# Hybrid attention layer on one core: the attention stage with values as weights, probabilities of four heads as the moving operand, and its query tiles run from the last to the first

## The chip, the cores and the metric

The kernel runs on 1 core of one Trainium2 chip. The metric is the device time of one execution in microseconds (us). Below, PE is TensorE (PEld its weight loads), DVE is VectorE, ACT is ScalarE, POOL is GpSimd, SP is SyncE, which here only issues DMAs.

## The reference, cut to what matters

One layer: a prompt of 1024 tokens and eight sequences that decode one token each. The change is in the attention of the prompt. For each query tile of 128 tokens, each of 8 heads (2 groups of 4 that share keys and values) and three branches, it computes a masked softmax over keys and multiplies by values; the three results are weighted by gates and summed.

```python
s_c = einsum('sghd,ngd->sghn', qg, kcb) * scale         # 63 compressed keys
p_c = masked_softmax(s_c, ...); o_c = einsum('sghn,ngd->sghd', p_c, vcb)
s_s = ... keys 0 .. query (all blocks are chosen at this length)
s_w = ... keys of the last 512 positions
o = g[..., 0:1] * o_c + g[..., 1:2] * o_s + g[..., 2:3] * o_w
mix = concat([o, retention_out], -1) @ w_out            # then the feed-forward part
```

## The kernel before, in words

Five stages follow one another, each a block with a barrier at its end: `stage_project` (twice), `stage_sequences` (the decoding sequences, and the compressed keys and values), `stage_attention` (the prompt's attention, here "the attention stage"), `stage_mix_out`, `stage_feed_forward`. There is no scheduler: each engine has its own list of instructions, written in order, with waits on semaphores.

The attention stage walks over *units*. A unit is one query tile, one head and one branch (compressed: 64 keys wide; selected: tile t has t+1 key tiles of 128; window: up to 5 key tiles). `attention_events` writes one order that all engines follow: S (scores of a unit, PE), T (transposes of up to four key tiles of one unit's probabilities, PE), V (values, PE). Behind S come the row maximum on DVE (`TENSOR_REDUCE`, L1683) and the exponential with its sum on ACT (L1618); behind T a copy of the transposed probabilities to SBUF, in turn on DVE (L1689) and ACT (L1633). In V the transposed probabilities are the weights (128x128, f32) and 64 columns of values move (L1586); f32 makes two PE instructions of each such product. The scores (L1554) are products of fp32r halves: a number is split into `hi` (ACT, L404) and `lo = x - hi` (L408). Each tile's outputs are scaled by gate / sum on POOL (L1661), summed over branches on DVE (L1712), transposed once more on PE (L1568) and kept in `mixT`. Banks: three sets for scores, 5 and 6 for T, 7 for V.

`keep_busy` (L400) issues products whose result nobody reads, at places where PE is about to wait.

## Time and profile before

| | |
|---|---|
| median of 3 runs | 2206.36 us (2204.49 to 2211.82) |
| the profiled execution | 2208.68 us, span of its instructions 2207.0 us |
| busy: PE, DVE, ACT, POOL | 2133.6, 775.0, 610.8, 467.1 us |
| PE instructions | 13245 |
| mean granted TensorE clock | 0.977 of 2.4 GHz |

PE is busy for almost the whole span. Busy time of PE is the union of modelled, overlapping intervals; what one instruction costs is read from the distance between starts.

### The profile page before, as it was taken

The numbers are of one execution on the slowest core, as the hardware profiler recorded it, in microseconds if no ns is written. First come the engines' busy times: TensorE is split into PE (matmuls) and PEld (weight loads), VectorE is DVE, ScalarE is ACT, GpSimd is POOL, SyncE is SP. The second block draws the span as 40 slices with busy tenths as digits, with TensorE's granted clock in tenths as the row PEclk, the third lists the DMA queues.
The fourth block names the chain that finished last, engine by engine and source line by source line (L and its number), as shares of the span: only waits on it lengthen the run. The fifth ranks groups of instructions, "written<-read, shape, count | busy, mean of one in ns | idle before, by whom it ended". The sixth has DMA issues, their size and how long they took to land. (4 is left out here: it accounts for less than half of the span.)

```text
span 2207.0 us, 35846 instructions
## 1 busy us (share of the span) xinstructions
PE 2133.6 (97%) x13245; PEld 1889.4 (86%) x13245; DVE 775.0 (35%) x1460; ACT 610.8 (28%) x1282; POOL 467.1 (21%) x424
## 2 busy tenths in 40 slices
PE   6999999989999999899999999999999999999998
PEld 5777768867777677789999998799999999999987
DVE  5544433554244444453544553301111011111015
ACT  4310111111343333354555552222110111111112
POOL 0111111212222331210100002133321333223330
PEclk9999989999999999986999999999999999999999
DMA  6211102247796774340000003221111111111123
GB/s 176 67 59 39 39 11 98 68 105 128 111 122 90 102 101 59 70 106 11 14 18 1 1 18 117 68 73 42 47 48 48 48 48 43 43 48 48 45 69 116
DMA packets 173859, 141.54 MB, mean 64 GB/s; under 512 B 16601, under 2 KB 160682, under 8 KB 173410
## 3 DMA queue, kind: packets, MB, share of 16 engines
q1 hardware_dynamic: 169634, 131.43, 26.0%
q0 software_dynamic: 4096, 8.40, 2.5%
q8 instruction: 80, 1.31, 0.3%
q14 instruction: 49, 0.40, 0.1%
HBM read 124.27 MB, written 19.69 MB: 65 GB/s over the span
## 5 line engine op out<-in xcount | busy, mean ns | idle before, releaser
L393 PE MATMUL banks<-halves 128*128 128x344 f32 (+4 forms) x5184 | 849.8, 326 | 2.5 <-POOL halves L408 2.5
L393 PEld LDWEIGHTS banks<-halves 128*128 128x128 f32 (+1 forms) x5184 | 816.4, 187 | 31.3 <-issue 2.8
L408 POOL TENSOR_TENSOR halves<-core,halves 128x1024 fp32r<-128x1024 f32 (+1 forms) x143 | 243.7, 1712 | 632.9 <-ACT halves L404 482.9
L393 PE MATMUL banks<-hidden 128*128 128x512 f32 (+3 forms) x1512 | 347.3, 385 | 4.3 <-DVE hidden L408 4.3
L393 PEld LDWEIGHTS banks<-hidden 128*128 128x128 f32 (+1 forms) x1512 | 252.8, 178 | 72.0 <-issue 4.6
L1065 PE MATMUL banks<-arena 128*128 128x254 f32 (+1 forms) x1152 | 245.3, 368 | 7.8 <-ACT arena L1201 7.8
L1065 PEld LDWEIGHTS banks<-arena 128*128 128x128 f32 x1152 | 206.4, 191 | 32.8 <-issue 6.1
L404 ACT ACTIVATE halves<-core 128x1024 fp32r<-128x1024 f32 (+1 forms) x85 | 88.0, 1047 | 389.5 <-PE banks L393 369.6
L1586 PE MATMUL banks<-kept,softmax 128*128 128x64 f32 (+1 forms) x1184 | 183.5, 289 | 7.8 <-ACT softmax L1633 4.9
L2046 DVE TENSOR_TENSOR core<-banks,core 128x344 f32<-128x344 f32 x66 | 34.1, 517 | 440.6 <-PE banks L393 440.6
L1586 PEld LDWEIGHTS banks<-kept,softmax 128*128 128x128 f32 (+1 forms) x1184 | 162.1, 203 | 17.6 <-issue 10.5
L1618 ACT ACTIVATE softmax<-banks,softmax 128x64 f32<-128x64 f32 (+8 forms) x192 | 109.4, 571 | 135.0 <-DVE softmax L1683 127.3
L1683 DVE TENSOR_REDUCE softmax<-banks 128x1 f32<-128x640 f32 (+4 forms) x184 | 102.4, 558 | 105.7 <-PE banks L1558 105.0
L1554 PE MATMUL banks<-pairs 128*128 128x128 f32 (+3 forms) x592 | 116.3, 325 | 1.3 <-DVE pairs L408 1.3
L966 POOL DMA_DIRECT2D arena<-in_cache_kv x128 | 67.8, 530 | 231.3 <-PE banks L1111 203.3
L1574 PE MATMUL banks<-core,softmax 128*128 128x128 f32 (+1 forms) x592 | 115.7, 292 | 0.0
L1554 PEld LDWEIGHTS banks<-pairs 128*128 128x128 f32 x592 | 99.3, 209 | 4.1 <-issue 1.5
L603 POOL TENSOR_TENSOR retention<-core,retention 128x256 f32<-128x256 f32 (+1 forms) x36 | 30.3, 842 | 260.9 <-ACT core L586 260.9
L400 PE MATMUL banks<-core 128*128 128x128 f32 x576 | 75.4, 297 | 9.9 <-PEq L132 3.8
L1689 DVE COPY softmax<-banks 64x128 f32<-64x128 f32 (+4 forms) x129 | 59.4, 460 | 72.5 <-PE banks L1574 71.8
L400 PEld LDWEIGHTS banks<-core 128*128 128x128 f32 x576 | 73.6, 212 | 10.7 <-issue 9.9
L1574 PEld LDWEIGHTS banks<-core,softmax 128*128 128x128 f32 (+1 forms) x592 | 77.3, 161 | 4.2
(213 smaller groups left out, 1887.3 us busy)
## 6 DMA issues: line engine op xcount, KB each, us to landing
core<-in_cache_kv SPq DMA_DIRECT2D x128, 128.0 KB, 5.5
core<-in_w_gate SPq DMA_DIRECT2D x22, 512.0 KB, 3.8
core<-in_w_up SPq DMA_DIRECT2D x22, 512.0 KB, 3.8
core<-in_x_prompt SPq DMA_DIRECT2D x16, 512.0 KB, 3.6
arena<-in_cache_kv SPq DMA_DIRECT2D x128, 64.0 KB, 5.5
arena<-in_cache_kv POOLq DMA_DIRECT2D x128, 64.0 KB, 5.3
retention<-in_w_in SPq DMA_DIRECT2D x16, 448.0 KB, 6.4
core<-in_w_down SPq DMA_DIRECT2D x16, 448.0 KB, 3.7
```

What stands on the lines that cost most here:

```text
L393: done = pe.matmul(out, left[a], right[b], start=(first and i == 0), stop=(last and i == 2))
L400: pe.matmul(m.banks[:, bank, 0:P], m.ident, m.ident, start=True, stop=True)
L404: return act.activation(hi, x, ACT.Copy)
L408: return engine.tensor_tensor(lo, x, hi.bitcast(F32), ALU.subtract)
L966: pool.dma_start(m.selv[16 * at:16 * at + 16, half, :, :], io.pool[bass.ds(page[pg], 1), :, :, 384:512].rearrange("a c t n -> (a c) t n")) ...
L1065: last = pe.matmul(m.banks[:, 2 + mt, 0:2 * nb], m.w1[kv][:, k, P * mt:P * mt + P], m.XT[:, k % 8, :, k // 8:k // 8 + nb], start=(k == 0), ...
L1554: last = pe.matmul(out[:, lo:hi], m.qs[t % 2][:, g, hh, :], pair[v][:, first + lo:first + hi], start=(v == 0), stop=(v == 1 and not mask))
L1574: last = pe.transpose(m.banks[0:w, 5 + i % 2, P * x:P * x + P], m.prob[u % 4][:, P * (first + x):P * (first + x) + w], m.ident)
L1586: last = pe.matmul(m.banks[:, 7, HD * (u % 8):HD * (u % 8) + HD], m.pts[i % 3][0:w, P * x:P * x + P], v[0:w, 64 * g:64 * g + 64], start=(f ...
L1618: act.activation(m.prob[i % 4][:, 0:width(i)], scores_of(i, width(i)), ACT.Exp, bias=m.nmax[:, i % 8:i % 8 + 1], accum_out=m.sums[UNITS[i] ...
L1683: dve.tensor_reduce(peak, out, AX.X, ALU.max, negate=True).then_inc(s["c_max"], 1)
L1689: dve.tensor_copy(m.pts[i % 3][0:w, 0:P * n], m.banks[0:w, 5 + i % 2, 0:P * n]).then_inc(s["c_kept_dve"], 1)
```

## The change

1. **Values as weights.** A turn (T) now takes one key tile of the four heads of a group: four transposes fill one bank with 512 columns. ACT rounds it to `hi`, DVE takes `lo`. V then has the weights `[value_hi | value_lo]` (128x128) and moves 512 columns twice (`hi`, `lo`). Bank 7 adds up all three branches of a group.
2. **Weights on the probabilities.** 1/sum and gate are multiplied into the probabilities before they are transposed, on POOL (`weigh`), per quad (four heads of one group and branch). The scaling of outputs, the sum over branches and the last transpose go; instead one half of bank 7 is copied by ACT, one by DVE, and POOL adds them.
3. **Order.** Units go (tile, group, branch, head), tiles from 7 to 0. Scores run 8 units ahead instead of 3, in two bank pairs (0-1, 2-3) instead of three; T uses banks 4 to 6, V runs two turns behind T.
4. **Preparation moved.** Splitting keys, the first two query tiles and the values, and the query loads, go from the start of the attention stage to the end of `stage_sequences`.
5. **All `keep_busy` calls are removed**, 288 products in 13 places of the run.

```diff
+VALUES = 2 * TP * 256 + 256
+PAIRS_C = 8 * SEQ + 2 * SEQ + 3 * 2 * 512 + VALUES
-UNITS = [(t, hh, g, br) for t in range(TP) for hh in range(4) for g in range(2) for br in range(3)]
-AHEAD = 3
-BANK_C = [4, 0, 2]
+UNITS = [(t, g, br, hh) for t in range(TP) for g in range(2) for br in range(3) for hh in range(4)]
+AHEAD = 8
+QUADS = len(UNITS) // 4
+def tile_at(x):
+    return TP - 1 - x
...
+    for k in range(QUADS):
+        n = key_tiles(4 * k)
+        for x in range(n):
+            turns.append((k, x, n))
+            events.append(("T", len(turns) - 1))
+            if len(turns) > 2:
+                values(len(turns) - 3)
+            while ahead < min(len(UNITS), AHEAD + 4 * k + -(-4 * (x + 1) // n)):
+                events.append(("S", ahead))
+                ahead += 1
...
     PE
-                    wait(pe, "c_exp", i - 2)
+                    wait(pe, "c_exp", i - 1)
...
+                    wait(pe, "c_lo", i - 2)
+                    pe.wait_ge(s["c_shared"], 4 * k + 4)
+                    for hh in range(4):
+                        last = pe.transpose(m.banks[0:w, 4 + i % 3, P * hh:P * hh + P],
+                                            m.prob[(4 * k + hh) % 12][:, P * x:P * x + w], m.ident)
...
-                        last = pe.matmul(m.banks[:, 7, HD * (u % 8):HD * (u % 8) + HD],
-                                         m.pts[i % 3][0:w, P * x:P * x + P], v[0:w, 64 * g:64 * g + 64],
+                    pe.wait_ge(s["c_lo"], i + 1)
+                    if br == 0:
+                        wait(pe, "c_out_act", k // 3)
+                        wait(pe, "c_out_dve", k // 3)
+                    for half in range(2):
+                        last = pe.matmul(m.banks[:, 7, :], v.rearrange("p v d -> p (v d)"), m.pts[i % 3][half][0:w, :],
...
     ACT: at S(i) exponent(i - 1); at T(i)
+                    act.wait_ge(s["c_turned"], i + 1)
+                    wait(act, "c_pv", i - 2)
+                    round_to_hi(act, m.pts[i % 3][0][0:w, :], m.banks[0:w, 4 + i % 3, :]).then_inc(s["c_hi"], 1)
...
     POOL
+                for hh in range(4):
+                    u, gate = 4 * k + hh, 12 * g + 3 * hh + br
+                    p = m.prob[u % 12][:, 0:width(u)]
+                    pool.tensor_scalar(p, p, m.share[t % 2][:, u % PER_TILE:u % PER_TILE + 1],
+                                       m.gates[:, tile_at(t), gate:gate + 1], ALU.mult, ALU.mult).then_inc(s["c_shared"], 1)
...
+                    if i % 4 == 1 and i >= 5:
+                        weigh((i - 5) // 4)
...
     DVE
+                    if i % 4 == 1 and i >= 5:
+                        inverse((i - 5) // 4)
+                    peak(i)
+                    low_halves()
...
     end of stage_sequences, on DVE (the three others stand before the copy to osm)
+                        dve.wait_ge(s["c_keys_hi"], 4)
+                        rest_to_lo(dve, m.keys[1][1][1], m.kstage[1][1], m.keys[1][1][0]).then_inc(s["c_keys_lo"], 1)
...
-                if q + 2 not in SEQS_B:
-                    keep_busy(pe, m, 2, 26 if q < NB_SEQ else 38)
...
-            keep_busy(pe, m, 7, 22)
```

On PE, in the attention stage before, for the last group of heads but one of tile 7 (L1574 is T, L1586 is V, L1554 and L1558 are S):

```order
1622 L1586 MATMUL banks<-kept,softmax 128x64
1623 L1574 MATMUL banks<-core,softmax 128x128 x4
1624 L1554 MATMUL banks<-pairs 128x512 x2
1625 L1554 MATMUL banks<-pairs 128x384 x2
1626 L1554 MATMUL banks<-pairs 128x128 x2
1627 L1558 MATMUL banks<-kept 128x128
1628 L1586 MATMUL banks<-kept,softmax 128x64
1629 L1574 MATMUL banks<-core,softmax 128x128 x4
1630 L1586 MATMUL banks<-kept,softmax 128x64 x4
```

After the change, on PE, in the first selected quad of tile 7 (L1561 is T, L1575 is V, L1549 and L1553 are S):

```order
638 L1561 MATMUL banks<-core,arena 128x128 x4
639 L1575 MATMUL banks<-pairs 128x512 x2
640 L1561 MATMUL banks<-core,arena 128x128 x4
641 L1575 MATMUL banks<-pairs 128x512 x2
642 L1549 MATMUL banks<-kept_pairs,pairs 128x64 x2
643 L1553 MATMUL banks<-kept 128x64
644 L1561 MATMUL banks<-core,arena 128x128 x4
645 L1575 MATMUL banks<-pairs 128x512 x2
646 L1561 MATMUL banks<-core,arena 128x128 x4
647 L1575 MATMUL banks<-pairs 128x512 x2
```

Four products of 64 moving columns have become two of 512 for four heads, and scores of the next compressed quad stand between every second pair of turns.

On POOL after the change, from the end of `stage_sequences` into tile 7 (L401 is the split to `lo`, L1627 `weigh`, L1649 the sum of a group's halves):

```order
634 L1009 CAST kept<-arena 128x128 x2
635 L401 TENSOR_TENSOR pairs<-arena,pairs 64x1024
636 L401 TENSOR_TENSOR pairs<-kept,pairs 128x16x64 x2
637 L401 TENSOR_TENSOR pairs<-kept,pairs 64x2x64
638 L401 TENSOR_TENSOR pairs<-arena,pairs 64x1024
...
642 L1627 TENSOR_SCALAR arena<-arena,kept 128x64 x4
643 L1627 TENSOR_SCALAR arena<-arena,kept 128x1024 x4
644 L1627 TENSOR_SCALAR arena<-arena,kept 128x640 x4
645 L1627 TENSOR_SCALAR arena<-arena,kept 128x64 x4
646 L1627 TENSOR_SCALAR arena<-arena,kept 128x1024 x4
647 L1649 TENSOR_TENSOR core<-core,arena 64x4x128
```

The splits of queries and values now stand ahead of the barrier, and each quad's probabilities pass through POOL.

## Rows read from the trace of the kernel before

**Rows 1.** The page: span, and granted clock in 40 slices of 55 us.
```profile
span 2207.0 us, 35846 instructions
...
PEclk9999989999999999986999999999999999999999
```

**Rows 2.** Busy time in the attention stage with its two ends (columns as named).
```profile
core 0: us, PE busy (x) PEld busy (x) DVE busy (x) ACT busy (x) POOL busy (x), PEclk, DMA share, GB/s
938.00:1316.00 378.00, 367.02 (x2901) 349.62 (x2902) 187.15 (x366) 194.95 (x556) 38.97 (x15) 0.92 0.09 22
```

**Rows 3.** The same inside the attention stage.
```profile
955.00:982.00 27.00, 25.28 (x216) 23.42 (x215) 15.81 (x58) 18.20 (x83) 5.11 (x2) 0.98 0.68 163
982.00:1036.00 54.00, 54.00 (x267) 51.46 (x266) 18.07 (x43) 21.25 (x69) 5.11 (x2) 0.51 0.06 17
1036.00:1310.00 274.00, 267.90 (x2269) 255.64 (x2269) 140.72 (x256) 147.63 (x392) 23.25 (x9) 1.00 0.02 7
```

**Rows 4.** Timeline of DVE: the instruction that closes a query tile, here tiles 0, 6, 7.
```profile
973.24 0.16 DVE L1695 TENSOR_SCALAR softmax<-softmax 128x24 f32<-128x24 f32 x1
...
1252.46 0.16 DVE L1695 TENSOR_SCALAR softmax<-softmax 128x24 f32<-128x24 f32 x1
...
1309.17 0.18 DVE L1695 TENSOR_SCALAR softmax<-softmax 128x24 f32<-128x24 f32 x1
```

**Rows 5.** Timeline of PE in tile 7: start, duration, line, count.
```profile
1291.00 1.23 PE L1554 MATMUL banks<-pairs 128*128 128x512 f32 x6
...
1292.23 0.43 PE L1586 MATMUL banks<-kept,softmax 64*128 64x64 f32 x2
1292.60 1.09 PE L1574 MATMUL banks<-core,softmax 128*128 128x128 f32 x8
1293.45 0.42 PE L1554 MATMUL banks<-pairs 128*128 128x128 f32 x2
...
1294.42 1.95 PE L1586 MATMUL banks<-kept,softmax 128*128 128x64 f32 x16
1296.21 0.28 PE L1574 MATMUL banks<-core,softmax 128*128 128x128 f32 x1
```

**Rows 6.** Busy time in 4 us of dense fp32r products of 512 columns (projection).
```profile
328.00:332.00 4.00, 4.00 (x19) 3.20 (x19) 1.47 (x3) 0.60 (x1) 1.14 (x2) 1.00 0.03 13
```

**Rows 7.** Groups by line and shape, DVE and ACT: count, busy us, mean ns.
```profile
L1683 DVE TENSOR_REDUCE softmax<-banks 128x1 f32<-128x640 f32 x40 | 33.0, 825 | 31.4 <-PE banks L1558 31.3
L1683 DVE TENSOR_REDUCE softmax<-banks 128x1 f32<-128x1024 f32 x8 | 9.8, 1223 | 7.0 <-PE banks L1558 7.0
L1618 ACT ACTIVATE softmax<-banks,softmax 128x640 f32<-128x640 f32 x40 | 31.7, 793 | 38.0 <-DVE softmax L1683 38.0
L408 DVE TENSOR_TENSOR halves<-banks,halves 128x512 fp32r<-128x512 f32 x16 | 10.2, 680 | 0.0
L404 ACT ACTIVATE halves<-banks 128x512 fp32r<-128x512 f32 x16 | 8.5, 582 | 0.0
```

**Rows 8.** The same for POOL: copies, and a subtraction of two tensors.
```profile
L986 POOL COPY arena<-core 128x2048 f32<-128x2048 f32 x16 | 32.0, 2010 | 98.7 <-DMA core<-in_cache_kv 70.3 <-PE banks L1044 28.4
L606 POOL COPY kept<-core 128x128 f32<-128x128 f32 x16 | 5.1, 318 | 0.0
L408 POOL TENSOR_TENSOR halves<-core,halves 128x1024 fp32r<-128x1024 f32 x76 | 182.9, 2408 | 474.4 <-ACT halves L404 474.4
```

**Rows 9.** Timeline where `stage_sequences` ends and the attention stage begins.
```profile
921.24 8.75 PE L400 MATMUL banks<-core 128*128 128x128 f32 x76 [0.36 <-ACT core L1192]
...
926.67 1.28 DVE L1355 TENSOR_SCALAR arena<-arena,core 8x2049 f32<-8x2049 f32 x1
...
936.97 0.22 PE L1117 MATMUL banks<-core,arena 8*128 8x8 f32 x1 [0.37 <-DVE arena L1362]
...
945.49 8.12 DVE L408 TENSOR_TENSOR pairs<-core,pairs 128x1024 fp32r<-128x1024 f32 x4 [7.92 <-ACT pairs L404]
...
955.34 0.27 PE L1574 MATMUL banks<-core,softmax 128*64 128x128 f32 x1
```

**Rows 10.** Timeline from the last V to the first product of `stage_mix_out`.
```profile
1308.54 1.28 PE L1586 MATMUL banks<-kept,softmax 128*128 128x64 f32 x10
...
1320.82 22.04 PE L393 MATMUL banks<-halves 128*128 128x512 f32 x96
```

More of the change, by code:

```diff
@@ L394, in split_products @@
     return done
-def keep_busy(pe, m, bank, n):
-    for _ in range(n):
-        pe.matmul(m.banks[:, bank, 0:P], m.ident, m.ident, start=True, stop=True)
 def round_to_hi(act, hi, x):
@@ L1453, in attention_events @@
[L1453 to L1474 removed]
+    turns, events, ahead = [], [("S", u) for u in range(AHEAD)], AHEAD
@@ L1477, in load_w_out, with turned_by @@
+    values(len(turns) - 2)
+    values(len(turns) - 1)
+    return turns, events
+TURNS_C, EVENTS_C = attention_events()
+def turned_by(k):
+    return sum(quad < k for quad, _, _ in TURNS_C)
 def load_w_out(sp, s, m, io, k):
```

395 lines of the change are left out of this document (170 added, 225 removed).

## The prediction, made before the changed kernel ran

> **What bounds the kernel now.** I read the page first: a span of 2207.0 us with a granted clock that is full nearly everywhere, but falls in two slices of the attention stage [rows 1]. Busy shares say little here, so the second view is busy time by stretch: in the attention stage PE is busy for 367 of 378 us, DVE and ACT for about half of it, POOL for a tenth [rows 2]. The mean clock there is 0.92, and the stretches inside show why: 54 us at 0.51 of 2.4 GHz, that is at the 1.2 GHz level, the rest at 2.4 GHz [rows 3]. So PE sets the pace, and the timeline gives its prices as distances between starts. In tile 7, eight transposes take 1293.45 - 1292.60 = 0.85 us, 0.106 each; sixteen V instructions 1296.21 - 1294.42 = 1.79 us, 0.112 each, and a key tile of a head needs two, 0.224; scores of 1024 keys take 1.23 us, window scores 0.97 us, compressed ones about 0.27 us (my estimate from the two) [rows 5]. Check: tile 7 has 8 x 14 key tiles, 112 x 0.330 = 37.0, plus 8 x 2.47 = 19.8, is 56.8 us; its closing instructions lie 1309.17 - 1252.46 = 56.7 us apart [rows 4]. A pure sum of PE work explains the tile.
>
> From the first T to the last V the stage takes 1309.3 - 955.3 = 354 us [rows 9, 10]. The 54 us at 1.2 GHz do the work of 27, so at full clock it would be 327. The PE sum over all eight tiles is 592 x 0.330 = 195, scores about 115 (from the prices above, falling with width to 0.3 for one key tile), last transposes 4: 314. The stage runs 4% above its sum.
>
> **V.** Removed are 592 x 0.224 = 132.6 us. Added are 148 turns x 2 products of 512 fp32r columns. The projection shows 19 such in 4.00 us, 0.21 each [rows 6]: 62.2 us. Transposes stay 592, scores stay. The last transposes and their wait go, -4. PE's own work at full clock falls from 327 to 327 - 70 - 4 = 253 us. On path, since PE was the bound.
>
> **The other engines get close.** A turn costs ACT a split of 512 columns (0.58) and DVE a subtraction (0.68); before, half the turns fell on each [rows 7]. For tile 7, DVE has 28 x 0.68 = 19, maxima 8 x (1.22 + 0.83 + 0.22) = 18, reciprocals and output copies 3: 40 us. ACT has 28 x 0.58 = 16, exponentials 8 x (1.12 + 0.79 + 0.31) = 18, others 2: 36. PE has 11.9 + 11.8 + 19.8 = 43.5. None exceeds PE, yet three engines at 80 to 100% that wait for one another in a fixed order don't overlap fully. Where I see waits:
> - Window scores now come four in a row behind the compressed turn, in two bank pairs, and S(i) waits for the exponential of i-2. One loop is 0.97 + 0.83 + 0.79 and some 0.2 of signals, 2.8 us for two, 1.4 each against 0.97: 1.7 us per group of heads, less for narrow tiles, 1.5 x 16 = 24 us. Queued behind the waiting S are the first transposes of the selected quad, and behind them ACT and DVE.
> - In the selected quad DVE takes a turn's low half behind the maximum of the next score, and T(i+2) waits for that half. Per two turns: max 0.22, low 0.68, T 0.44, V 0.42, S 0.27, signals 0.3, is 2.3 against 2.0 of PE work: 0.15 x 72 turns = 11 us.
> - The first V of a group waits until both halves of bank 7 are copied (about 0.6 us) with only one T ahead of it: 0.5 x 16 = 8 us.
> - `weigh` on POOL is an operation no row shows: one tensor and two per-partition factors. Nearest is POOL's copy, also of one tensor: 2.01 us for 2048, 0.32 for 128 columns, so 1.1 for 1024; the far bound is the subtraction of two tensors, 2.41 [rows 8]. Nothing lets it cost less than a copy. It lies on the path once a group: for the selected quad it starts some 2.65 us after that quad's last scores (max 1.22, exponential 1.12, signals and reciprocal), and PE has 7.3 us of other work until it needs the result (two turns 1.7, four window scores 5.6). At the copy's price 2.65 + 4 x 1.1 = 7.1: hidden, barely. At the subtraction's, 12.3: 5 us per group in tile 7. I take the copy's, since the engine reads one tensor, and 5 us in all for what doesn't fit.
>
> The Trainium skill (GPSIMD Engine Reference, 3.1) gives about 2.6 cycles per element with two inputs and 1.8 at 1.2 GHz as best for a tight loop; by the latter, an estimate from that page, 1024 columns would take some 1.7 us and the total would be about 11 us higher. The copy in this trace is faster than that page's 1.8, and the subtraction's 2.4 us agree with its 2.6.
>
> Stage: 253 + 24 + 11 + 8 + 5 = 301 against 354, -53 us. This includes that the long 1.2 GHz stretch isn't repeated (27 us of it): it began on narrow tile 1 and ended as the tiles grew wider, and the new order begins with wide ones. That part is the least certain.
>
> **Preparation moved.** Before, T begins at 955.34, 18.4 us after PE's last work of the stage ahead, most of it behind DVE's four splits of keys (8.12 us) [rows 9]. After, those run in the tail of `stage_sequences`. They aren't free: the last selected exponential stands behind four splits on ACT (+1.2), DVE does a split ahead of the last output copy (+1.4 to 2.1), POOL subtracts two query and two value tiles, 2.4 each, starting about 928 when ACT gives the first: its end is near 942 instead of 937. On the other side the transposes that waited for `keep_busy` until 929.99 could start at 927.95 (-2.0). First S at about 942.7. Eight scores before the first T cost some 4 us more than their PE work, a cold start 3, the first `weigh` 1: -5 us net. The drain of the last quads adds 4.
>
> **The idle-time products.** 288 x 0.23 = 66 us of PE time go, but nearly all lay in waits, so I count none as gain but the 2.0 above. The one ahead of that, 26 products, hid nothing and kept the clock: without it PE idles 6 us and the following 7 us of work may run at 1.2 GHz, +3. At the start of `stage_mix_out` PE waits for POOL's first low half as before: 11.0 us from last V to first product [rows 10] become 2.7 (copy, sum, barrier) + 4.9 + 3 cold = 10.6: 0. The other places: cold start against an earlier start, 0; if that cover is missing, 1 to 3 us each for six places.
>
> **Sum.** -53 - 5 + 4 + 3 + 0 = -51. The profiled execution took 2208.7; 2157.7. The runs' median lies 2.3 below it: 2156 us.
>
> **The rivals.**
> - *Clock, slower than before.* PE stops several times per group now. At 1.2 GHz tile 7's PE work is 87 us against 51 forecast, so each us spent there loses about 0.4. The forecast gain is used up by some 120 us more at 1.2 GHz than I assume. For it: before, the clock fell within tile 1 and stayed low for 54 us though PE was 100% busy there [rows 3], and nothing fills the waits now. Against: wide tiles ran at 2.4 GHz for 274 us, the work was narrow where it fell, and V now moves 512 columns for each load. If it decides: 2215 to 2260. 12%. The Trainium skill (TensorE: Matmul & The Clock Gate, 1) says idle gaps cool the engine; that the clock fell behind waits here agrees.
> - *POOL at the two-tensor price.* 5 us per group in tile 7 falling to nothing in tile 0 is 40 us, and the window quad adds 2 for eight groups: about +50, 2205 us, no change. 8%.
> - *Waits hidden.* If running 8 ahead hides nearly all waits, the stage takes its PE sum, 255 to 265: 2115 us. 10%.
> - *The forecast*, 2120 to 2190: 67%. The rest (3%) is spread.
>
> **How the numbers follow.** A difference of 0.3%, about 7 us, is what the measurement can tell. Faster: 67 + 10 and half of what ends between 2190 and 2205, 5, is 82%; same 5%; slower 13%. The range 2110 to 2210 takes in the two-tensor bound and the hidden case and leaves out the clock rival and a little below.
>
> **What would show it.** V: 296 instructions at distances of 0.21 us, tile 7 in about 51 us. Scores: starts of consecutive window scores 1.4 us apart, PE released by ACT. `weigh`: 1.1 us for 1024 columns; a PE wait on POOL ahead of the first selected transposes would prove it longer. Clock: a row of 0.5 inside tiles 7 to 3 would prove me wrong. The boundary: first S near 943, last V near 1256. The forecast fails most likely if PE's waits are longer than these loops, or if the clock follows them.

## The result, and the profile after

The changed kernel takes 2200.02 us (median of 11 runs, 2198.84 to 2206.69), the kernel before 2207.79 us in the same rounds (11 runs, 2204.09 to 2213.43). The ratio is 0.9966 with a 95% interval of 0.9954 to 0.9979: faster by 0.34%, some 7.5 us, where the forecast was 51. The time lies in the range, but the likeliest case was wrong by 44 us. Its profiled execution took 2200.3 us. In the rounds of some later experiments five executions of the kernel before took only 2179 to 2185 us, at a mean granted clock of 0.990 to 0.993 where the others have 0.975 to 0.983; that is some 27 us less, about what its low stretch costs (none of the five has a trace), and it widens several of the intervals below.

On the page of the changed kernel, TensorE's busy time and the granted clock in 40 slices (before: [rows 1]):

```profile
PE 2037.4 (93%) x11749; PEld 1762.2 (80%) x11749; DVE 810.0 (37%) x1526; ACT 642.4 (29%) x1290; POOL 597.8 (27%) x628
...
PEclk9999989988999999789889769999999999999999
```

The attention stage begins in the 18th slice and ends in the 24th. The kernel before showed two slices below 9 there, now there are five, and a sixth just ahead of the stage. Busy time by stretch, with the sum of PE's instructions in parentheses behind it and the granted clock third from the end, here from the first T to the last V:

```profile
core 0: us, PE busy (x) PEld busy (x) DVE busy (x) ACT busy (x) POOL busy (x), PEclk, DMA share, GB/s
955.10:1300.70 345.60, 297.00 (x1794) 252.94 (x1793) 205.71 (x418) 213.29 (x541) 153.96 (x209) 0.85 0.05 14
```

The same tile by tile, 7 to 0 (each stretch ends where GpSimd adds the last group of the tile, L1649):

```profile
955.00:1022.70 67.70, 57.09 (x363) 49.55 (x361) 42.21 (x70) 42.77 (x92) 27.29 (x31) 0.90 0.14 37
1022.70:1076.20 53.50, 47.87 (x302) 41.22 (x300) 34.66 (x62) 34.89 (x78) 22.99 (x28) 0.88 0.04 11
1076.20:1127.80 51.60, 46.77 (x283) 39.83 (x281) 32.16 (x59) 32.19 (x76) 22.09 (x28) 0.85 0.04 11
1127.80:1171.20 43.40, 37.80 (x249) 32.22 (x249) 29.16 (x58) 29.82 (x74) 21.28 (x28) 0.96 0.08 25
1171.20:1207.90 36.70, 29.27 (x208) 25.59 (x208) 24.47 (x53) 25.60 (x70) 19.56 (x28) 1.00 0.01 2
1207.90:1245.70 37.80, 32.15 (x188) 27.80 (x188) 19.75 (x50) 22.44 (x66) 17.84 (x28) 0.77 0.00 1
1245.70:1279.30 33.60, 28.44 (x148) 24.09 (x148) 15.43 (x49) 17.33 (x61) 13.70 (x27) 0.70 0.00 1
1279.30:1301.00 21.70, 17.72 (x61) 12.73 (x61) 8.16 (x28) 8.65 (x32) 9.20 (x18) 0.50 0.00 1
```

From these rows the whole miss can be worked out. The length of a stretch is PE's busy time and its idle time. The busy time multiplied by the granted clock is what the same work takes at 2.4 GHz, the rest of it is what the low clock costs. Summed over the eight tiles, this is 252.4 us of work at 2.4 GHz, 44.8 us for the clock and 48.9 us of idle time; by the one row ahead of them it is 252.5, 44.6 and 48.6, the numbers used below. The forecast had 253 of work, 48 of waits and nothing for the clock. (The clock has two decimals, so each such product is good to 1 or 2 us.) The kernel before, by the row from its first T to its last V (354.50 us, PE busy for 346.68, clock 0.92), spends 318.9, 27.7 and 7.8 us. So V's cheaper form returns 66 us, the waits take 41 back and the clock 17 more.

How a fall of the clock looks from close by: TensorE in stretches of 2 us in tile 6, where a group of heads changes.

```profile
1038.00:1040.00 2.00, 1.60 (x12) 1.52 (x12) 0.94 (x2) 1.58 (x3) 0.00 (x0) 1.00 0.00 0
1040.00:1042.00 2.00, 1.02 (x10) 0.91 (x8) 1.95 (x4) 0.89 (x2) 0.35 (x1) 1.00 0.00 0
1042.00:1044.00 2.00, 1.74 (x13) 1.64 (x14) 1.08 (x2) 0.92 (x3) 2.00 (x3) 0.94 0.00 0
1044.00:1046.00 2.00, 0.94 (x5) 0.75 (x3) 0.82 (x1) 0.84 (x2) 1.94 (x2) 0.50 0.00 0
1046.00:1048.00 2.00, 1.91 (x8) 1.75 (x8) 0.00 (x0) 0.60 (x1) 0.00 (x0) 0.50 0.03 8
1048.00:1050.00 2.00, 2.00 (x10) 1.38 (x8) 1.59 (x4) 1.91 (x5) 1.11 (x1) 0.50 0.00 0
```

PE is busy for 1.60, 1.02 and 1.74 of 2 us, and at 1043.8 us the level falls to 1.2 GHz. It holds to 1054.0: through one more wait of 1.15 us, for GpSimd, and 8 us in which PE is fully busy. Such waits are paid twice: once as idle time, once as slow work behind them. In steps of 0.25 us the level falls seven times in tiles 7 to 4. Four times (965.3, 992.5, 1019.8 and 1074.5 us) this comes at the end of a wait of 1.3 to 2.1 us for GpSimd or within 2 us behind it; three times (here, at 1098.3 and at 1146.3) it comes ahead of that wait, behind waits of scores for ScalarE. Not every wait is paid twice: tile 3 has the largest share of idle time of all eight, 7.4 of 36.7 us, in waits of 1.0 us at most, and its clock is 1.00. Who ends these waits, from the waits of PE between 940 and 1310 us (in total, times, longest):

```profile
PE banks L1549 <- ACT arena L1593: 27.9, 51, 1.4
PE banks L1561 <- POOL arena L1627: 16.9, 21, 2.1
PE banks L392 <- POOL halves L401: 7.3, 1, 7.3
PE banks L1549 <- PEq L890: 3.5, 1, 3.5
PE banks L1575 <- DVE pairs L401: 2.4, 7, 0.6
PE banks L1561 <- DVE pairs L401: 2.0, 2, 1.0
```

Scores (L1549) wait for the exponential (L1593), the first selected turn (L1561) for `weigh` (L1627). The price of `weigh`, the operation that no row of before showed, from the groups by shape (count, then busy us and mean ns):

```profile
L1627 POOL TENSOR_SCALAR arena<-arena,kept 128x640 f32<-128x640 f32 x40 | 34.4, 874 | 15.3 <-DVE arena L1679 14.7
L1627 POOL TENSOR_SCALAR arena<-arena,kept 128x64 f32<-128x64 f32 x64 | 24.0, 393 | 87.9 <-DVE arena L1679 87.9
...
L1627 POOL TENSOR_SCALAR arena<-arena,kept 128x1024 f32<-128x1024 f32 x8 | 9.4, 1195 | 13.6 <-DVE arena L1679 13.6
```

1.195 us for 1024 columns: near the copy's price (1.1 taken), far from the subtraction's 2.41. The Trainium skill (GPSIMD Engine Reference, 3.1) has 1.8 cycles per element as the best case of a tight loop, from which I had estimated 1.7 us. From 64 to 1024 columns the rows give 0.84 ns a column, 1.0 cycle at that section's 1.2 GHz; that disagrees with the 1.8 and is near the 1.03 that the same section has for bodies bound by the read and write ports. The measurement decides.

### The profile page after: what moved, and what is told of

The parts are those of the page before. It is cut to its first block and busy times, and to the rows that moved or that the text cites. A ratio compares the mean times of both kernels' runs of the same rounds, so it can differ in the third digit from the quotient of the medians.

```text
span 2198.6 us, 32717 instructions
## 1 busy us (share of the span) xinstructions
PE 2037.4 (93%) x11749; PEld 1762.2 (80%) x11749; DVE 810.0 (37%) x1526; ACT 642.4 (29%) x1290; POOL 597.8 (27%) x628
## 5 line engine op out<-in xcount | busy, mean ns | idle before, releaser
L401 POOL TENSOR_TENSOR halves<-core,halves 128x1024 fp32r<-128x1024 f32 (+1 forms) x143 | 243.8, 1713 | 575.5 <-ACT halves L397 425.6
L1085 PE MATMUL banks<-arena,blocks 128*128 128x254 f32 (+1 forms) x1152 | 248.1, 372 | 9.7 <-ACT arena L1219 5.7
L1085 PEld LDWEIGHTS banks<-arena,blocks 128*128 128x128 f32 x1152 | 209.2, 194 | 35.1 <-issue 6.1
L2037 DVE TENSOR_TENSOR core<-banks,core 128x344 f32<-128x344 f32 x66 | 34.1, 517 | 439.8 <-PE banks L392 439.8
L1627 POOL TENSOR_SCALAR arena<-arena,kept 128x64 f32<-128x64 f32 (+8 forms) x192 | 122.2, 652 | 164.2 <-DVE arena L1679 162.9
L1668 DVE TENSOR_REDUCE arena<-banks 128x1 f32<-128x64 f32 (+8 forms) x184 | 102.3, 556 | 103.1 <-PE banks L1553 102.5
L1549 PEld LDWEIGHTS banks<-pairs 128*128 128x128 f32 x592 | 103.0, 204 | 36.7 <-issue 27.1
L1549 PE MATMUL banks<-pairs 128*128 128x128 f32 (+3 forms) x592 | 109.2, 315 | 20.8 <-ACT arena L1593 20.5
L1593 ACT ACTIVATE arena<-banks,arena 128x64 f32<-128x64 f32 (+8 forms) x192 | 109.1, 568 | 60.1 <-DVE arena L1668 56.2
L1575 PE MATMUL banks<-pairs 128*128 128x512 f32 (+1 forms) x296 | 122.5, 500 | 3.4 <-DVE pairs L401 2.4
L1561 PE MATMUL banks<-core,arena 128*128 128x128 f32 (+1 forms) x592 | 107.2, 311 | 19.0 <-POOL arena L1627 16.9
L397 ACT ACTIVATE pairs<-banks 128x512 fp32r<-128x512 f32 (+1 forms) x148 | 88.3, 596 | 85.3 <-PE banks L1561 84.6
L401 DVE TENSOR_TENSOR pairs<-banks,pairs 128x512 fp32r<-128x512 f32 (+1 forms) x148 | 100.0, 680 | 9.9 <-ACT pairs L397 9.9
L1561 PEld LDWEIGHTS banks<-core,arena 128*128 128x128 f32 (+1 forms) x592 | 74.5, 157 | 28.3 <-issue 18.9
```

The source lines that it names most:

```text
L397: return act.activation(hi, x, ACT.Copy)
L401: return engine.tensor_tensor(lo, x, hi.bitcast(F32), ALU.subtract)
L1085: last = pe.matmul(m.banks[:, 2 + mt, 0:2 * nb], m.w1[kv][:, k, P * mt:P * mt + P], m.XT[:, k % 8, :, k // 8:k // 8 + nb], start=(k == 0), ...
L1549: last = pe.matmul(out[:, lo:hi], m.qs[t % 2][:, g, hh, :], pair[v][:, first + lo:first + hi], start=(v == 0), stop=(v == 1 and not mask))
L1561: last = pe.transpose(m.banks[0:w, 4 + i % 3, P * hh:P * hh + P], m.prob[(4 * k + hh) % 12][:, P * x:P * x + w], m.ident)
L1575: last = pe.matmul(m.banks[:, 7, :], v.rearrange("p v d -> p (v d)"), m.pts[i % 3][half][0:w, :], start=(br == 0 and half == 0), stop=(br ...
```

## The experiments

All ratios are to the kernel before, run on the same chip in the same rounds; its medians there lie between 2207.4 and 2210.4 us. The experiments are compared with one another and with the changed kernel (2200.02 us) by their medians, across rounds. For each kernel the stretch from the first T to the last V is split as above, in its one profiled execution. Where idle-time products stand inside the loop, they are part of the work. The profiled execution of `earlier` is the shortest of ten (2200.0 us), that of earlier_fill the longest of four (2187.9 us), so their splits look better and worse than their medians.

| kernel | us, median | ratio, 95% interval | first T to last V | work at 2.4 GHz | clock | idle |
|---|---|---|---|---|---|---|
| before | 2207.79 | 1 | 354.5 | 318.9 | 27.7 | 7.8 |
| changed | 2200.02 | 0.9966, 0.9954 to 0.9979 | 345.6 | 252.5 | 44.6 | 48.6 |
| bare_before | 2228.49 | 1.0092, 1.0063 to 1.012 | 370.3 | 316.8 | 47.3 | 6.1 |
| old_fill | 2215.25 | 1.0028, 1.0012 to 1.0043 | 345.2 | 253.3 | 41.2 | 50.7 |
| first_to_last | 2208.15 | 1.0, 0.9983 to 1.0017 | 355.3 | 254.9 | 48.5 | 51.9 |
| fill_inside | 2182.86 | 0.9897, 0.9862 to 0.9932 | 328.8 | 293.9 | 9.1 | 25.8 |
| fill_half | 2181.82 | 0.9911, 0.987 to 0.9952 | 330.0 | 281.2 | 18.0 | 30.8 |
| fill_both | 2174.59 | 0.9874, 0.9833 to 0.9914 | 328.0 | 283.4 | 11.8 | 32.8 |
| weigh_short | 2163.65 | 0.9858, 0.9751 to 0.9965 | 308.2 | 252.2 | 21.9 | 34.1 |
| spread | 2261.72 | 1.0312, 1.0199 to 1.0425 | 403.7 | 248.9 | 66.2 | 88.7 |
| earlier | 2210.56 | 1.0019, 0.999 to 1.0047 | 344.7 | 253.6 | 37.9 | 53.2 |
| dve_one | 2207.75 | 1.0003, 0.9977 to 1.0029 | 349.6 | 252.5 | 44.6 | 52.5 |
| earlier_fill | 2182.31 | 0.9896, 0.9831 to 0.9962 | 338.1 | 282.7 | 21.3 | 34.1 |
| earlier_dve_fill | 2186.85 | 0.9907, 0.9877 to 0.9936 | 337.2 | 284.5 | 15.0 | 37.7 |
| prompt | 2167.75 | 0.985, 0.9798 to 0.9902 | 313.6 | 251.0 | 21.8 | 40.7 |
| prompt_fill | 2164.56 | 0.9828, 0.9759 to 0.9897 | 316.4 | 278.0 | 11.6 | 26.8 |
| prompt_fill_win | 2159.02 | 0.9804, 0.9735 to 0.9873 | 308.2 | 269.5 | 8.3 | 30.4 |
| banks4 | 2199.55 | 0.9948, 0.9924 to 0.9972 | 345.6 | 248.3 | 47.3 | 50.0 |
| prompt_banks4 | 2162.21 | 0.978, 0.9758 to 0.9802 | 307.1 | 247.6 | 15.8 | 43.7 |
| best | 2155.62 | 0.9763, 0.9743 to 0.9783 | 307.4 | 262.4 | 13.8 | 31.2 |

The work column is the check on the method: in the ten kernels that have the changed loop and no products in it, it is 248 to 255 us, while the stretch itself takes 307 to 404 us. What differs is the clock and the waits.

The expectations speak of "low-clock time": the time at the 1.2 GHz level, which is 2 x (1 - clock) x length. For the changed kernel it is 2 x 0.15 x 345.6, about 104 us (the expectations say 103).

**bare_before: the kernel before without its idle-time products.**

```
 def keep_busy(pe, m, bank, n):
-    for _ in range(n):
-        pe.matmul(m.banks[:, bank, 0:P], m.ident, m.ident, start=True, stop=True)
+    return
```

> The kernel before with all of its idle-time products (288 of them) left out and nothing else changed. Theory A (the chip lowers TensorE's clock where TensorE waits often or long, and these products kept it up at the stage boundaries): low-clock rows appear behind the boundaries and in stage_mix_out, and the time rises by 6 to 20 us to 2214 to 2228. Rival N (my forecast: the products were worth nothing): within 3 us of before, 2205 to 2211. The attention stage itself has no such products between its first and last turn, so by both it stays near 354 us from first T to last V.

Slower by 0.92%, some 20 us: my zero for these products was wrong. Most of the loss is where I did not look. First T to last V takes 370.3 us instead of 354.5, although none of the products taken out stood in that stretch; both readings had it unchanged. By stretch:

```profile
942.00:1051.00 109.00, 97.62 (x476) 92.33 (x477) 43.12 (x108) 47.40 (x161) 15.68 (x6) 0.50 0.23 57
1051.00:1326.00 275.00, 268.87 (x2274) 256.49 (x2273) 141.56 (x257) 148.30 (x393) 23.25 (x9) 1.00 0.03 7
...
955.70:1051.00 95.30, 95.30 (x467) 90.42 (x468) 34.26 (x100) 41.11 (x153) 10.22 (x4) 0.50 0.23 56
```

Without the products at the entry of the stage the clock is at the 1.2 GHz level for 109 us from the first score on, with PE busy for 97.6 of them, and from the first T on (the last row) for all 95.3; in [rows 3] it was 54. So a low clock is not only a matter of the gap just ahead: once low, it stayed low through the narrow tiles 0 and 1 and into tile 2 although PE was never idle, and rose as the tiles grew wide.

**old_fill: the changed kernel with the products at their old places.**

```
+            keep_busy(pe, m, 7, 38)
             for what, i in EVENTS_C:
+                if (what, i) == ("T", 0):
+                    keep_busy(pe, m, 7, 18)
...
+            keep_busy(pe, m, 7, 22)
             for i in range(NT + 1):
```

> The changed kernel with the idle-time products put back at all places where the kernel before had them, none inside the attention loop. Theory A: the granted clock inside the attention stage stays near 0.85, since its waits are not filled; the stretch 1300 to 1431 goes from 0.91 back to 1.00 and stage_sequences from 0.95 to 0.98; the time falls by 8 to 16 us, to 2184 to 2192. Rival N: 2197 to 2203. Rival O (the low clock inside the attention stage is a consequence of how it is entered): the stage's clock rises to 0.92 or more and the time falls by over 20 us, to below 2180.

It is slower than without them, against all three readings, and the timeline of PE at the entry of the stage says why:

```profile
942.65 0.22 PE L1151 MATMUL banks<-core,arena 8*128 8x8 f32 x1 [3.40 <-DVE arena L1411]
947.80 11.41 PE L399 MATMUL banks<-core 128*128 128x128 f32 x76 [4.93 <-PEq L900]
...
968.75 5.07 PE L399 MATMUL banks<-core 128*128 128x128 f32 x36
```

The 38 products (76 records, two to a product) take 11.4 us, the 18 ahead of the first T 5.1 us. The wait of 18 us that they filled in the kernel before is gone, since the preparation was moved, so 16 us of them lie on the path. Inside the loop nothing changed (clock 0.86). A product that fills a wait has to go when the wait goes; but from where the first product of `stage_mix_out` runs to the end, this kernel needs 885.9 us instead of the changed kernel's 890.6, so the late ones are worth some 5 us, less 2 by which that first product is itself delayed.

**first_to_last: the order of the tiles alone.**

```
 def tile_at(x):
-    return TP - 1 - x
+    return x
```

> The changed kernel with the query tiles taken from the first to the last again (one line). Theory A: the waits are in every tile, so low-clock stretches appear in the wide tiles again, now late in the stage; order alone is worth less than 8 us: 2192 to 2208. Rival T (it is the order that lowers the clock: narrow tiles in the last 80 us, and a cold start on wide ones): the clock of the stage moves by 0.04 or more and the time by over 15 us, in either direction.

8 us slower than the changed kernel, with nearly the same clock (0.84 against 0.85) and idle time within 4 us.

```profile
954.90:1060.00 105.10, 86.75 (x428) 72.94 (x428) 44.84 (x125) 53.06 (x172) 44.68 (x75) 0.65 0.16 40
1060.00:1310.20 250.20, 216.66 (x1384) 185.83 (x1382) 163.53 (x289) 163.15 (x369) 109.98 (x134) 0.93 0.02 7
```

The order moves the low stretch of the narrow tiles from the end to the start and does not make it. The order is not the cause, and my hope that "the new order begins with wide ones" would save the 27 us was without ground.

**fill_inside and fill_half: products in the loop's waits.**

```
                 if what == "S":
...
+                    keep_busy(pe, m, 4 + turned % 3, {0: 0, 1: 0, 2: 2}[br])
                     wait(pe, "c_exp", i - 1)
...
                 elif what == "T":
...
                     wait(pe, "c_lo", i - 2)
+                    turned = i + 1
+                    if x == 0:
+                        keep_busy(pe, m, 4 + i % 3, (0, 4, 0)[k % 3])
                     pe.wait_ge(s["c_shared"], 4 * k + 4)
```

They write the bank that the next turn will overwrite. fill_half has 1 and 3 in place of 2 and 4.

> The changed kernel with idle-time products inside the attention loop only: 2 ahead of each window score and 4 ahead of the first selected turn of a group, 192 products of 128 columns, 44 us at 2.4 GHz, placed where the trace shows TensorE waiting for ACT and for POOL. Theory A (TensorE's many short waits lower its clock): granted clock of the stage 0.97 or more, the 45 us that the low clock costs come back less some 10 to 20 us of products that do not fit into the waits: 2165 to 2175. Rival W (the clock falls for another cause, such as narrow tiles or load): clock stays near 0.85 and the products cost 10 to 25 us: 2210 to 2225.

> Idle-time products inside the attention loop as in the run with 192 of them, but 1 ahead of each window score and 3 ahead of the first selected turn: 112 products, 26 us at 2.4 GHz. With 192, the low-clock time from first T to last V fell from 103 to 18 us, and 19 of their 44 us lay on TensorE's path. Theory A (short waits lower the clock, and fillers that just fit restore it): low-clock time stays under 30 us, under 8 us of products on the path, time 2168 to 2178. Rival D (the clock needs the whole filling): low-clock time above 60 us, time 2185 to 2198.

This is the direct test of the clock. With 192 products more work and nothing else changed, the kernel is faster by 17 us, and the clock inside the stage shows one low stretch, in the narrow tiles:

```profile
953.40:1247.00 293.60, 272.95 (x2013) 242.03 (x2011) 191.67 (x371) 198.03 (x485) 140.73 (x181) 1.00 0.06 17
1247.00:1282.20 35.20, 30.09 (x167) 25.18 (x166) 14.14 (x47) 15.47 (x57) 14.03 (x29) 0.74 0.00 1
```

The clock's part falls from 44.6 to 9.1 us. The work grows by 41 us (192 products at 0.23 us would be 44); 23 of them went into waits (idle 48.6 to 25.8) and 18 or 19 onto the path. That is within the 10 to 20 expected, but the clock gave back 35.5 us and not all 45, and the time lies 8 us above the range. With 112 products the clock holds less well (18.0) and less lies on the path (28.7 us more work, 17.8 less idle time): the same time, between the two readings. So idleness was the cause of the falls in the wide tiles, and filling is a dear cure.

**fill_both: with products at the ends of the neighbouring stages.** fill_half, and `keep_busy` as before in `values` (26 and 38), 14 in place of 22 at the start of `stage_mix_out`, 14 at its end, 18 at the start of the feed-forward stage.

> The 112 products inside the attention loop as in the run with half the filling, and products where the kernel before had them around the last two values of stage_sequences (26 and 38), at the start (14 instead of 22) and the end (14) of stage_mix_out and at the start of the feed-forward stage (18), none at the start of attention and none in the projections. Theory A: 3 us less up to the first score, 3 us less in stage_mix_out and behind it than the run with the 112 alone. Rival N (these outer products are worth nothing by themselves, as between the kernel before with and without them up to 895 us): the same time as that run within 2 us.

7 us below fill_half by the medians. The two profiled executions differ by 5.0 us: 3.0 from the first product of `stage_mix_out` to the end, 2.0 from the first T to the last V, nothing elsewhere. The products at the end of `stage_sequences` gave nothing by the first T.

**weigh_short: GpSimd's work cut.** Only 64 columns of each row are weighed, the rest is left out.

```
-                    p = m.prob[u % 12][:, 0:width(u)]
+                    p = m.prob[u % 12][:, 0:64]
```

> The changed kernel with GpSimd's weighing of the probabilities cut to the first 64 columns of each score row (the rest stays unweighed, so part of the computation is left out). Theory P (the wait of the first selected turns for GpSimd, 16.9 us in 21 places, is a cause of its own and also starts the clock's falls in the wide tiles): these waits go, low-clock time falls by 20 us or more, time 2165 to 2182. Rival L (another wait of the loop takes their place, the scores' wait for the exponentials above all): 2188 to 2200, with the clock of the stage near 0.85.

```profile
PE banks L1549 <- ACT arena L1593: 28.4, 54, 1.4
...
PE banks L1561 <- POOL arena L1627: 1.9, 4, 0.7
```

The wait for GpSimd falls from 16.9 to 1.9 us, the scores' wait stays. The stage gets 37 us shorter: 15 of idle time and 23 of clock. The time, 2163.65 us, is 1 us below theory P's range. GpSimd's lateness, which I had at 5 us, costs 37. From the first T up to 1150 us the level still falls four times, behind waits of scores, and stays low for 3.3 to 3.5 us each time; in the changed kernel it falls seven times up to there, for 3.3 to 10.3 us.

**spread: the window scores spread over the selected turns.**

```
-            while ahead < min(len(UNITS), AHEAD + 4 * k + -(-4 * (x + 1) // n)):
+            upto = 4 * k + (2 if k % 3 == 0 else -2 + -(-6 * (x + 1) // n) if k % 3 == 1 else -(-4 * (x + 1) // n))
+            while ahead < min(len(UNITS), AHEAD + upto):
```

> The changed kernel with the window scores spread: two of the four behind the compressed turn, the other two and the next compressed scores over the selected turns, instead of four in a row. Theory S (my term of 24 us: four window scores in a row wait for maximum and exponential through two bank pairs, 27.9 us of waits in 51 places): these waits fall to under 12 us, and the time by 8 to 20 us, to 2180 to 2192. Rival P (the first selected turn then comes earlier and waits that much longer for GpSimd's weights): TensorE's wait for GpSimd grows from 17 to 30 us or more, and the time stays within 6 us of 2200.

```profile
PE banks L1562 <- POOL arena L1628: 73.9, 28, 5.6
PE banks L1550 <- ACT arena L1594: 12.7, 26, 1.2
```

The scores' waits fell to 12.7 us, nearly what theory S had, and the time rose by 61 us. The wait for GpSimd grew as in rival P, but to 73.9 us, and the time left P's range as well, which was 2200 within 6 us. The four window scores in a row are the cover under which GpSimd weighs. In the sum, 57 us more waiting for GpSimd and 15 less for ScalarE made 40 us more idle time and 22 more of clock loss.

**earlier and dve_one: two ways to help GpSimd.** `earlier` makes the four selected scores one window turn sooner; `dve_one` gives the fourth selected head to VectorE, behind the maximum of the fourth window score.

```
+            steps = max(1, n - 1) if k % 3 == 2 else n
-            while ahead < min(len(UNITS), AHEAD + 4 * k + -(-4 * (x + 1) // n)):
+            while ahead < min(len(UNITS), AHEAD + 4 * k + min(4, -(-4 * (x + 1) // steps))):
```

```
-                for hh in range(4):
+                for hh in range(3 if br == 1 else 4):
...
                     peak(i)
+                    if i % 4 == 3 and i >= 7 and UNITS[i - 7][2] == 1:
+                        weigh_last((i - 7) // 4)
```

> The changed kernel with the four selected scores of the next group placed one window turn earlier (behind the first turns of the window quad but its last), so that GpSimd starts to weigh them earlier; nothing else. Cutting GpSimd's weighing to 64 columns took 15 us of waits and 54 us of low clock from the stage, 37 us in all; spreading the scores the other way cost 58. Theory P (GpSimd misses its due time by about 1 us a group, and each miss also lowers the clock in the wide tiles): TensorE's wait for GpSimd falls from 17 to under 8 us, low-clock time from 103 to under 75, time 2172 to 2188. Rival R (the earlier scores wait for the exponentials of their own predecessors instead, so the chain starts no earlier): 2196 to 2204.

> The changed kernel with one of the four selected heads weighed by VectorE (behind the maximum of the fourth window score) instead of GpSimd. Theory P: GpSimd's chain is 1.2 us shorter in the widest tile, the wait of the first selected turn for it nearly goes (under 6 us in all) if VectorE is in time, low clock under 75 us, time 2172 to 2190. Rival V (VectorE is the next late one: its 1.1 us ahead of a low half delays turns and the wait moves there): within 6 us of 2200, with the first selected turn waiting for VectorE.

> The earlier selected scores together with the 112 products inside the loop and those at the ends of the neighbouring stages (2174.6 us without the earlier scores). Theory P: once the wait for GpSimd is short, the products ahead of the selected turns do not fit into it any more (48 of them, 11 us), so the two edits do not add up: 2164 to 2174. Rival: they add, the wait gains 10 us or more again: below 2162.

> Earlier selected scores, one selected head weighed by VectorE, and the same products. Theory P: no wait for GpSimd left, and the time of the run without VectorE's share within 5 us, since what it could still remove is under 5 us: 2160 to 2172. Rival V (VectorE's extra 1.1 us a group delays low halves): 5 us or more above the run without it.

None helped: `earlier` and `dve_one` can't be told from the kernel before, their medians are 11 and 8 us above the changed kernel's and outside every range that was put down for them, and with the products they are 8 and 12 us above fill_both. In dve_one the first selected turn waits for VectorE's weighing instead (21.3 us in 16 places), which is the mechanism of rival V. In `earlier` the wait for GpSimd stays at 19.3 us, so how early the scores are made does not set its start. In the changed kernel, the last selected score of the group of the 2 us stretches above, on PE:

```profile
1035.52 1.03 PE L1549 MATMUL banks<-pairs 128*128 128x512 f32 x6
1036.39 0.23 PE L1553 MATMUL banks<-kept 128*128 128x128 bf16 x1
...
1046.09 1.09 PE L1561 MATMUL banks<-core,arena 128*128 128x128 f32 x4 [1.15 <-POOL arena L1627]
```

its exponential on ACT:

```profile
1038.00 0.59 ACT L397 ACTIVATE pairs<-banks 64x512 fp32r<-64x512 f32 x1 [0.31 <-PE banks L1561]
1038.50 0.99 ACT L1593 ACTIVATE arena<-banks,arena 128x896 f32<-128x896 f32 x1
```

the maximum of the first window score, a low half, and only then the reciprocal on DVE:

```profile
1040.05 0.82 DVE L1668 TENSOR_REDUCE arena<-banks 128x1 f32<-128x640 f32 x1 [1.11 <-PE banks L1553]
1040.79 0.67 DVE L401 TENSOR_TENSOR pairs<-banks,pairs 64x512 fp32r<-64x512 f32 x1
1041.39 0.16 DVE L1679 RECIPROCAL arena<-arena 128x4 f32<-128x4 f32 x1
```

and GpSimd:

```profile
1041.65 4.29 POOL L1627 TENSOR_SCALAR arena<-arena,kept 128x896 f32<-128x896 f32 x4 [6.97 <-DVE arena L1679]
```

`weigh` starts 5.2 us after the last instruction of the last selected score (1036.4 to 1041.65). The exponential ends at 1039.5, but its sum is inverted behind a maximum whose score PE has not yet made. The program writes exponential i at event S(i+1) and the reciprocal at the second event S behind the quad, so both hang on the next scores.

**prompt: two places in the queues.** The last selected exponential goes right behind its own score on ScalarE, the reciprocal ahead of the first window score's maximum on VectorE. No work is added or taken away.

```
+def last_selected(u):
+    return UNITS[u][2] == 1 and u % 4 == 3
+def sums_ready(i):
+    if i % 4 == 0 and i and last_selected(i - 1):
+        return i // 4 - 1
+    if i % 4 == 1 and i >= 5 and not last_selected(i - 2):
+        return i // 4 - 1
...
-                    if i:
+                    if i and not last_selected(i - 1):
                         exponent(i - 1)
+                    if last_selected(i):
+                        exponent(i)
...
-                    if i % 4 == 1 and i >= 5:
-                        inverse((i - 5) // 4)
+                    if sums_ready(i) is not None:
+                        inverse(sums_ready(i))
```

> The changed kernel with its scores where they are, but the exponential of the last selected head queued on ScalarE right behind its own score instead of one score later, and the reciprocal (and so GpSimd's weighing) of the selected quad ahead of the first window score's maximum and low half instead of behind them. In the trace the weighing starts 5.2 us after the last selected score, of which 1.7 us is the reciprocal queued behind that maximum and low half. Theory Q (GpSimd is late because its start hangs on a place in the queues, not on when the scores are made, which is why making them earlier changed nothing): it starts 1.3 to 1.8 us earlier, TensorE's wait for GpSimd falls from 17 to under 6 us, low-clock time in the stage from 103 to under 80, time 2170 to 2188. Rival R (ScalarE now stands in that exponential while a turn's high half waits, and the wait moves to the turns): 2195 to 2208.

```profile
PE banks L1563 <- ACT arena L1607: 28.2, 49, 1.4
...
PE banks L1575 <- POOL arena L1643: 6.4, 12, 1.0
```

2167.75 us is 32 us below the changed kernel and 2 us below the range of theory Q. The wait for GpSimd falls from 16.9 to 6.4 us, idle time by 8, and the clock's part from 44.6 to 21.8. Theory Q had the wait under 6 us and the low-clock time under 80 (it is 50). On DVE the reciprocal now stands ahead of the window's maximum, and GpSimd starts behind it, 3.9 us after the last selected score (1032.4 to 1036.3):

```profile
1036.07 0.17 DVE L1695 RECIPROCAL arena<-arena 128x4 f32<-128x4 f32 x1
1036.15 0.80 DVE L1684 TENSOR_REDUCE arena<-banks 128x1 f32<-128x640 f32 x1
```

```profile
1036.34 4.31 POOL L1643 TENSOR_SCALAR arena<-arena,kept 128x896 f32<-128x896 f32 x4 [5.61 <-DVE arena L1695]
```

The two moves were only run together, so what each gives is not known.

**prompt_fill and prompt_fill_win: products on top of it.** The first has all of fill_both, the second the same without the 3 ahead of each first selected turn.

> The same, with the 112 products inside the loop and those at the ends of the neighbouring stages (2174.6 us without the prompt start). Theory Q: what the prompt start takes away was partly filled already, so 2160 to 2170. Rival R: 2174 to 2184.

> The same without the 3 products ahead of each first selected turn (64 products inside the loop). Theory Q: those 48 products (11 us) stood in a wait that is gone, so leaving them out saves 4 to 9 us against the run with them, if the clock holds: 2154 to 2164. Rival (the clock falls without them): equal or above the run with them.

Both in the ranges of theory Q: with GpSimd prompt, the 48 products cost 5.5 us and the clock holds without them.

**banks4, prompt_banks4, best: the score banks.** A score row of up to 512 columns takes one of the four banks, a wider one a pair.

```
-        b = 2 * (u % 2)
-        return m.banks[:, b:b + 2, :].rearrange("p a n -> p (a n)")[:, 0:width(u)]
+        b = BANKS_OF[u]
+        return m.banks[:, b[0]:b[-1] + 1, :].rearrange("p a n -> p (a n)")[:, 0:width(u)]
...
-                    wait(pe, "c_exp", i - 1)
+                    wait(pe, "c_exp", FREE_AT[i])
```

> The changed kernel with score banks given out by width: a score row of up to 512 columns takes one of the four banks instead of a pair, so that up to four such scores are in flight; rows over 512 columns take a pair as before. Theory S (my term of 24 us: scores wait for the exponential two back because there are two pairs): the waits of scores for ScalarE, 28 us, fall to under 15 us, mostly in tiles 3 to 0, whose low clock shortens too: 2182 to 2194. Rival L (another engine's pace sets these tiles, so the wait only moves): 2197 to 2203.

> Banks by width together with the prompt start of GpSimd (2167.8 us without the banks). Theory S: 6 to 16 us less, 2152 to 2162. Rival L: 2165 to 2170.

> Banks by width, the prompt start, the 64 products ahead of window scores and those at the ends of the neighbouring stages (2159.0 us without the banks). Theory S: the products ahead of the window scores no longer stand in waits in the narrow tiles, so less is left to gain: 2150 to 2157. Rival L: 2157 to 2161.

```profile
PE banks L1579 <- POOL arena L1645: 36.0, 23, 2.8
PE banks L1567 <- ACT arena L1611: 12.4, 20, 1.0
```

In banks4 the scores' wait falls from 27.9 to 12.4 us, and the wait for GpSimd rises from 16.9 to 36.0: the time does not move. My term of 24 us was a real wait, but behind it stood another that took it over. With the prompt start the banks give 5.5 us, between the two readings. `best` (banks by width, prompt start, 64 products in the loop, those at the neighbouring stages' ends) takes 2155.62 us, 0.9763 of the kernel before: 2.4% faster and in theory S's range, where the change alone gave 0.34%. That this is the time I forecast for the change is chance.

## Why the prediction was wrong, point by point

**V: right in sum.** The forecast had 253 us of PE work at full clock, the row gives 252.5. V has 296 instructions. But a turn with its two V products takes 0.90 to 0.95 us against my 0.86: its four transposes 0.35 to 0.39 us instead of 0.44, its two products 0.55 instead of 0.42. Over 148 turns that is 6 to 13 us more than forecast, so that the whole fits to 1 us is in part luck; which of the other terms was too high by as much is open.

**The waits: right in sum, wrong in their parts.** 48 us forecast, 48.6 measured, which is luck, since three of the four terms were far off. The scores' wait for ScalarE was 24 and is 27.9. The low halves were 11 and are 4.4 (2.4 and 2.0), the first V of a group 8 and is under 1. GpSimd was 5 and is 16.9. There the step that failed is that "for the selected quad it starts some 2.65 us after that quad's last scores". I added up the durations of its chain and left out what the program's order puts ahead of the exponential and the reciprocal on their engines; it starts 5.2 us after them. The price per row, over which I drew the rival of 8%, was right (1.195 us for 1024 columns), so POOL's late start did what its price did not.

**The clock: the step that failed.** The stage's sum "includes that the long 1.2 GHz stretch isn't repeated (27 us of it)" and counts every wait at its own length, so the low clock stands in the sum at nothing. Measured are 44.6 us of clock loss, which is the miss: 301 + 44.6 is 345.6, the stage's length. fill_inside shows the cause for the wide tiles by adding work alone, and weigh_short and prompt show that half of the loss hangs on GpSimd's late start: prompt took away 8 us of idle time and 23 us of clock loss. The order of the tiles has no part in it (first_to_last).

**The clock rival** named the mechanism and its price (0.4 us for each us at 1.2 GHz; 44.6 / 104 is 0.43) and needed some 120 us more at that level than I assumed to decide. There were about 104 in the stage, so it ate most of the gain and not all. I held it at 12% and read its evidence wrongly: against it I had put that wide tiles ran at 2.4 GHz for 274 us [rows 3], but those were wide tiles in which PE was busy for 267.9 of 274 us, and the forecast itself put waits into them. The Trainium skill (TensorE: Matmul & The Clock Gate, 1) says idle gaps cool the engine; fill_inside agrees, with 44.6 us of clock loss down to 9.1. Idle gaps are not the whole of it: in bare_before PE was busy for 95.3 of 95.3 us at the 1.2 GHz level.

**Preparation moved: wrong by its 5 us.** The first score stands at 944.16 (forecast 942.7):

```profile
940.42 0.22 PE L1135 MATMUL banks<-core,arena 8*128 8x8 f32 x1 [0.44 <-DVE arena L1395]
944.16 0.38 PE L1549 MATMUL banks<-kept_pairs,pairs 128*128 128x64 f32 x2 [3.52 <-PEq L890]
```

The first T is at 955.1, as in [rows 9]. PE's last work of `stage_sequences` moved from 937.0 to 940.4, and the four splits of keys took 2.74 us each on DVE instead of the 2.03 of [rows 9].

**The idle-time products: wrong.** Counted at nothing; in the kernel before they are worth 20 us (bare_before), mostly through the clock of the stage behind them. In the changed kernel the ones at the ends of the neighbouring stages are worth a few us (fill_both), the ones at the entry of attention cost 16 (old_fill).

**The start of `stage_mix_out`.** Its first product starts 7.3 us after the last V ended, where [rows 10] gave 11.0 and I had 10.6; the stage then runs 2.9 us longer, at a clock of 0.97 instead of 1.00.

**Sum.** The span fell from 2207.0 to 2198.6 us: 0.2 up to the first T, 8.9 in the stage, 3.7 from the last V to the next product, less 4.4 behind it.

**Left open.** Why the narrow tiles run at the low level even where PE is busy: in every profiled kernel without products in the loop some of the narrow tiles are low, and with 192 products the last 35 us still stand at 0.74. Nothing here separates the width of the work from the gaps around it. Why tile 3, with the largest share of idle time, kept its clock, while tiles 5 to 7 did not, is open too. What is left of the waits in `best` (31 us) was not followed further; the three engines' shares and the order are the next thing to plan.

## What to carry to other kernels

When a change makes the bounding engine's work shorter, price its new waits twice, as idle time and as slow work behind them, unless a row shows the clock holding with such waits: here 48.6 us of waits came with 44.6 us of clock loss. That is a first guess to plan with and not a law: prompt_banks4 had 43.7 us of waits and 15.8 of clock loss, and the kernel before 7.8 and 27.7. Count a chain by what stands ahead of each link in its engine's queue, not by the links' durations, and look for a due time in the order before moving work between engines: two instructions of each group, moved by one place, gave 32 us, where a quarter less work for the late engine and earlier input for it gave nothing. Idle-time products belong to the wait they fill; remove or move them with it.

## What the runs showed of the hardware that I had not expected

- Three waits of 0.26 to 0.98 us, 1.7 us together within 6 us, stood ahead of the fall to the 1.2 GHz level at 1043.8 us; it rose at 1054.0, with one wait of 1.15 us in between. Such waits once a group came with a mean of 0.85 to 0.90 in tiles 7 to 5, in which PE was busy for 84% of the time or more, while tile 3, with PE busy for 80%, stood at 1.00.
- At the entry of the stage in bare_before the level stayed at 1.2 GHz for 109 us, in the last 95.3 of which PE was never idle; with 56 products at that entry the low stretch was 54 us.
- Adding 192 products, 44 us of work, to the engine that sets the pace made the kernel 17 us faster.
- GpSimd's multiplication of one tensor by two per-partition factors took 0.393 us for 64 columns and 1.195 us for 1024.
